# Thirty-two more tokens fetched instead of computed densely, in a decoder step with product-key experts

## The chip, the cores and the metric

The kernel is one program on one NeuronCore of a Trainium2 chip. The number that counts is the device time of one execution in microseconds (us). The engines are PE (TensorE, matrix products), PEld (its weight loads, which run beside the products), DVE (VectorE), ACT (ScalarE), POOL (GpSimd, here nothing but an issuer of indirect DMAs) and SP (SyncE, the issuer of plain DMAs).

## The reference

One decoder layer for 560 token rows: 32 "sample" rows (8 running sequences of 4 tokens, each with 16 cache pages of 128 past tokens) and 528 prompt rows (16 of them meta tokens). What matters here, in outline:

```python
z   = h @ w_in                                # projections
mix = [MLA attention (8 heads), mLSTM (4 heads, 128 x 128 state)] @ w_out
h   = layer_norm(alpha * h + mix)
q   = h @ w_query                             # 8 heads x 2 halves x 128
s1, s2 = q1 @ keys1.T, q2 @ keys2.T           # 128 keys each
top 16 of s1 and s2, top 16 of their 256 sums -> 16 experts of 16384 per head, gates by softmax
y   = sum over the 128 chosen experts e of gate_e * gelu(h . u_e) * v_e
out = layer_norm(alpha * h + y)
```

The experts' tables u and v are 16384 x 1024 in fp32. All outputs (tokens, caches, mLSTM states) are fp32.

## The kernel before

**Two ways to the experts.** The 560 rows stand in five tiles of R = (80, 128, 96, 128, 128) rows; tile 2 (ST) begins with the 32 sample rows. Tiles 0 and 1 are group 0, tiles 2 to 4 group 1. 192 tokens of group 0 (64 of tile 0 and the 128 of tile 1) *fetch* their experts' rows: POOL issues an indirect DMA for one slot of all partitions (`fetch`, L1478: 128 rows of 4 KB, 512 KB), DVE multiplies and sums it with the token (`dot`, L1650 early and L2064 late) and later, for the v rows, scales and adds it (`early_add` L2079, `add_rows` L2071). The 64 tokens stand in the partitions twice, so that they take 64 slots of two experts; tile 1 takes 128 slots. That makes 192 fetches of u rows and 192 of v rows, through a ring of RING = 6 buffers. The 16 meta rows of tile 0 need no output.

The 352 rows of group 1 are computed *densely* against all 16384 experts, in 128 blocks of 128 experts. For each block PE makes the up product (L1024: 8 pieces of the depth x 3 products of rounded and remainder parts, each 352 columns wide), ACT the gelu, DVE `gated` (L2053, times the gates of the block), ACT the rounded part hh, DVE the remainder hl (`low_hidden`, L2057), and PE the down product (L1034: for each of three tiles, three products hh x vh, hh x vl, hl x vh, each in two halves of 512 columns, 18 matmuls in all). ACT rounds u and v (L1129), DVE makes their remainders (`low_u` L2043, `low_v` L2047). The first HS = 24 up products are done early in fp32 (L986), between the gate products.

**The order of the program.** Each engine has its own list, held together by semaphores.

1. Projections (L634), keys and choices of group 0 (`best_keys`, `choose`).
2. Attention of group 1's first tile beside the attention of the samples: `attention(ST, TI - 1, samples=True, each=U_SAMPLE)`. Before it stand `rotate_queries(1)`, `forget_gates(1)` (waits for ACT L1200, L1201) and `sample_queries` (L1618 to L1627, signals qs_ready). For each sample PE computes the scores (L778, L782, L785, L786; the signal is sm_s, for which DVE L1871 waits) and the values (L803 to L809; signal sm_o). After sm_o of sample b the pages of sample b + 2 are loaded: SP loads SP_PAGES = 12 of 16 (L481), POOL gathers the other 4 and 4 pieces of the rotary keys (L1483, L1486), and U_SAMPLE = 5 u rows beside (L1478).
3. `old_states` (mLSTM of the samples) with U_OLD = 11 dots, further tiles, output products with U_OUT = 15, expert queries and keys (L970) with U_KEYS = 24 dots in sets of `best_keys` and 6 dots.
4. Gate stage: for each four tokens DVE makes one-hots (L2036, L2038), PE multiplies them to a matrix of gates (L1011), ACT copies it to a stage buffer (L1129), and SP stores 32 tokens at a time (a chunk, NCH = 11 of them) to a DRAM table `gates`. SP reads it back in quads of four blocks (L521).
5. Down stage and loop: first the 24 early blocks (down products alone, `early_gated` L2085), then 13 turns of 8 blocks (`eight`). Five of the turns have LATE = 18 late dots and 6 adds (24 fetches), eight have 18 adds (18 fetches).
6. Layer norms (LN, L1548 to L1555) of the five tiles on DVE one after the other, each after its residual add (L2232, L2236), and the stores.

Of the kernel before, what the change touches and what calls it, by code (L numbers as in the profile page):

```python
# [6 lines left out]
ALU = mybir.AluOpType  # L7
# [4 lines left out]
U32 = mybir.dt.uint32  # L12
# [9 lines left out]
R = (80, 128, 96, 128, 128)  # L22
T = (0, 80, 208, 304, 432)
# [4 lines left out]
G0 = (0, 208)  # L28
GW = (208, 352)
LAST = (63, 127, 95, 127, 127)  # L30
NF = 64
NH, NOPE, ROPE, VD = 8, 64, 32, 64
# [13 lines left out]
FSETS = (NF, SLOTS)  # L46
RING = 6
CHUNKS = 11
LATE = 18
SP_PAGES = 12  # L50
ITER = LATE * 4 // 3
U_SAMPLE = 5
U_OLD = 11
U_TILE = 4
U_OUT = 15
U_KEYS = 24
U_PRE = SB * U_SAMPLE + U_OLD + 3 * U_TILE + U_OUT + U_KEYS
U_LOOP = 5
HS = 24
HS_GAP = 9  # L60
HS_TURN = 2
V_EARLY = 6 * HS // 8
# [18 lines left out]
HID = 5864  # L81
# [18 lines left out]
assert TS0 + 3592 <= SK0  # L100


def build(nc, x, consts, vecs, lnin, ln1, ln2, wts, w_qb, w_uk, w_uv, sub_keys,
          eu, ev, ur, vr, cache, kpet, pages, ct0, nt0,
          o_y, o_ckv, o_kpe, o_c, o_n, o_m, o_cs, o_ns):
    with ExitStack() as ctx:
# [53 lines left out]
        rstd, rs1, rs4 = small(TI), small(1), small(MH)  # L160
# [22 lines left out]

        hid = view(HID, TI, D)
        lnv = view(LNV, 2, D)
# [16 lines left out]
        class Attention:  # L202

            def __init__(self, at, g):
# [17 lines left out]
                at = max(at, XB + 2 * KD * 512 + 464) if g else at  # L222
# [13 lines left out]
        assert att[0].end <= HTA and att[1].end <= SK0  # L236
# [7 lines left out]
        assert XA + CA <= SK0 and EB + CA + 2 * 544 <= LNV + 2 * D + 64  # L244
# [8 lines left out]
        sc = [view(WQB, 8, NK), view(ZONE, 16, NK)] + [view(ZONE + n * 16 * NK, 16, NK) for n in range(3)]  # L253
        scB = view(ZONE, 3, 16, NK)
        sv = [view(LNV + n * 512, 16, TOPK) for n in (0, 1, 0, 1, 2)]
        siu = [view(LNV + n * 512 + 256, 16, TOPK).bitcast(U32) for n in (0, 1, 0, 1, 2)]
# [8 lines left out]
        cf = view(TS0 + 2944, SLOTS)  # L265
        cb = view(TS0 + 3072, SLOTS)
        ca = view(TS0 + 3200, 2, SLOTS)
        cau = view(TS0 + 3456, SLOTS).bitcast(U32)
# [6 lines left out]
        ZT = XB - 960  # L275
# [15 lines left out]
        assert SCE + D <= ZT  # L291
# [25 lines left out]
        hh = [rounded(f"hh{p}", TS0 + 2 * D + p * GW[1], GW[1])[:, :] for p in range(2)]  # L317
        hl = [rounded(f"hl{p}", TS0 + 2 * D + (2 + p) * GW[1], GW[1])[:, :] for p in range(2)]

        def as32(ap):  # L320
# [15 lines left out]
            "y_ps acc_in out_tok out_state out_y").split()}  # L336
# [26 lines left out]
        def z_bank(at):  # L363
            return 4 + (at - ZB[1]) % 3 if ZB[1] <= at < z_end(1, 4) else at % 4

# [50 lines left out]
        def _(sp):  # L416
# [47 lines left out]
            for n in range(7, 13):  # L464
                chunk(n)
                if n == 9:
                    sp.wait_ge(s["ht_ps"], TI + 1)
                    sp.dma_start(hid[NF:128, 0, :], hid[0:NF, 0, :]).then_inc(s["dup_in"], 16)
# [54 lines left out]

            def load_early_u(pair):
                sp.dma_start(ue[pair % 2].rearrange("p a d -> p (a d)"), eu[pair]).then_inc(early_in[pair % 2], 16)
# [16 lines left out]
            for c in range(NCH):  # L542
# [3 lines left out]
                if c == (T[TI - 1] - S0) // CH + 1:  # L546
# [7 lines left out]
                    load_early_a(1)  # L554
                sp.wait_ge(s["ev_done"], CH // 4 * (c + 1))
                sp.dma_start(gates[c * NK:(c + 1) * NK, :], stage[c % 2].rearrange("p e t -> p (e t)")).then_inc(gs_in[c % 2], 16)
            load_v(1, 1)
            sp.wait_ge(gs_in[0], 16 * ((NCH + 1) // 2))
            sp.wait_ge(gs_in[1], 16 * (NCH // 2))
            for q in range(2):  # L560
                load_gates(q, q)
# [32 lines left out]

            sp.wait_ge(s["f_done"], 2 * sum(FSETS))
            sp.wait_ge(s["y_ps"], NK)
            sp.dma_start(ring[0][0:NF, :], hid[NF:128, 0, :]).then_inc(s["acc_in"], 16)
            for n, i in enumerate((1, 2, 3, 4)):
                sp.wait_ge(s["ln_done"], 2 * TI + n + 1)
                sp.dma_start(o_y[tile(i), :], hid[0:R[i], i, :]).then_inc(s["out_y"], 16)  # L600
            sp.wait_ge(s["ln_done"], 3 * TI)
# [1760 lines left out]
```

## Time and profile before

| what | value |
|---|---|
| median of 3 runs | 2148.72 us (2138.95 to 2148.87) |
| profiled execution | 2147.01 us |
| its span (first to last instruction) | 2145.1 us |
| granted TensorE clock, mean | 0.904 |
| busy: PE, DVE, ACT, POOL | 89%, 67%, 28%, 27% |
| DMA traffic | 479.29 MB, mean 223 GB/s |

The profiled execution is one run with the profiler's records; 1.9 us of its time lie outside the span. Clock 1.00 is 2.4 GHz, 0.5 is 1.2 GHz. A row of the timeline gives start, duration, engine, line, operation, output tile and input tiles, and in brackets the idle time before it and who ended it. "remote" and "another core or an unknown queue" stand where the profile finds no releaser; here there is one core only.

### The profile page before, as it was taken

To read this page: it belongs to the slowest core of one execution; us is meant where nothing else is said; L and a number is where in the kernel's file an instruction comes from. 1 tells how busy PE (TensorE), PEld (TensorE's weight loads), DVE (VectorE), ACT (ScalarE), POOL (GpSimd) and SP (SyncE) were. 2 spreads that over 40 slices of the span, in tenths; PEclk is the share of its full clock that TensorE was granted. 3 is DMA by queue.
4 is the path that set the end of the run, shared out by engine and by line. 5 is a ranking of instruction groups with operands and counts; after the bars stand their busy time and mean duration, and the time that the engine had idled before them with its cause. 6 is when DMAs were issued, how large, how long until landed. Compare 5 with 4: busy or idle time off the path is not lost.

```text
span 2145.1 us, 26500 instructions
## 1 busy us (share of the span) xinstructions
PE 1915.8 (89%) x9117; PEld 1500.0 (70%) x9117; DVE 1436.1 (67%) x3189; ACT 609.1 (28%) x1020; POOL 586.6 (27%) x454
## 2 busy tenths in 40 slices
PE   6988899666688988999886999999999999999994
PEld 3556674554467745667675788888888888888883
DVE  4025366243346755999986778888888777777777
ACT  1132122210011111114455333333333333333331
POOL 0000002344423123310000114454454444444440
PEclk9989999666675679999998999999999999999997
DMA  6611334354534456554438878999998888888872
GB/s 250 228 40 40 123 118 162 108 164 146 186 137 147 148 171 229 202 178 149 164 141 302 295 278 321 356 349 340 364 340 301 317 289 291 320 287 292 318 255 92
DMA packets 152645, 479.29 MB, mean 223 GB/s; under 512 B 14624, under 2 KB 75856, under 8 KB 130928
## 3 DMA queue, kind: packets, MB, share of 16 engines
q1 hardware_dynamic: 94704, 270.60, 34.8%
q0 software_dynamic: 57856, 207.65, 27.2%
q8 instruction: 43, 0.70, 0.1%
q14 instruction: 42, 0.34, 0.0%
HBM read 443.73 MB, written 33.94 MB: 223 GB/s over the span
## 4 chain that ended last, share of the span: by engine, by line
PE 73%; DVE 16%; another core or an unknown queue 4%; DMA 3%; issue 2%; ACT 2%; POOL 0%; SPq 0%; DVEq 0%; ACTq 0%
PE ps L1034 24%; PE ps L1024 19%; PE ps L634 6%; PE ps L970 3%; PE ps L935 3%; PE ps L986 3%; DVE lo L1650 2%; PE ps L1011 2%; PE ps L721 2%; PE ps L720 2%; PE ps L803 2%; PE ps L743 1%; PE ps L638 1%; DMA lo<-x 1%
## 5 line engine op out<-in xcount | busy, mean ns | idle before, releaser
L1478 POOL DMA_INDIRECT lo<-ur,lo x192 | 244.3, 1272 | 797.8 <-DVE lo L2011 323.5
L1478 POOL DMA_INDIRECT lo<-vr,lo x192 | 278.1, 1448 | 650.1 <-DVE lo L2079 306.7
L1024 PE MATMUL ps<-xh,uh 128*128 128x352 f32 x832 | 270.6, 325 | 0.0
L1024 PE MATMUL ps<-xh,ul 128*128 128x352 f32 x832 | 270.5, 325 | 0.0
L1024 PE MATMUL ps<-xl,uh 128*128 128x352 f32 x832 | 268.8, 323 | 0.0
L1129 ACT ACTIVATE hi<-ps 128x512 f32<-128x512 f32 (+10 forms) x259 | 154.3, 645 | 373.7 <-PE ps L970 111.9
L1034 PE MATMUL ps<-vh,hh 128*128 128x512 f32 (+1 forms) x768 | 240.9, 395 | 19.9 <-DVE vl L2047 19.9
L1034 PE MATMUL ps<-vl,hh 128*128 128x512 f32 (+1 forms) x768 | 241.1, 395 | 0.0
L1034 PE MATMUL ps<-vh,hl 128*128 128x512 f32 (+1 forms) x768 | 240.0, 394 | 0.0
L2071 DVE SCALAR_TENSOR_TENSOR lo<-lo 128x1024 f32<-128x1024 f32 x174 | 221.8, 1282 | 18.5 <-DMA lo<-vr,lo 9.7
L2047 DVE TENSOR_TENSOR vl<-hi,vh 128x1024 fp32r<-128x1024 f32 x128 | 156.9, 1226 | 48.8 <-ACT vh L1129 48.3
L1034 PEld LDWEIGHTS ps<-vh,hh 128*128 128x128 f32 (+1 forms) x768 | 138.1, 180 | 48.3 <-issue 20.5
L1129 ACT ACTIVATE hh<-hi 128x352 fp32r<-128x352 f32 x128 | 63.7, 498 | 364.1 <-PE ps L1034 275.1
L1034 PEld LDWEIGHTS ps<-vl,hh 128*128 128x128 f32 (+1 forms) x768 | 138.4, 180 | 39.8 <-issue 0.2
L1034 PEld LDWEIGHTS ps<-vh,hl 128*128 128x128 f32 (+1 forms) x768 | 138.2, 180 | 39.9 <-issue 0.2
L1024 PEld LDWEIGHTS ps<-xl,uh 128*128 128x128 f32 x832 | 156.3, 188 | 4.5
L1024 PEld LDWEIGHTS ps<-xh,uh 128*128 128x128 f32 x832 | 156.3, 188 | 4.3
L2057 DVE TENSOR_TENSOR hl<-hi,hh 128x352 fp32r<-128x352 f32 x128 | 67.3, 526 | 135.2 <-ACT hh L1129 135.2
L1024 PEld LDWEIGHTS ps<-xh,ul 128*128 128x128 f32 x832 | 155.9, 187 | 0.0
L634 PE MATMUL ps<-hi,lo 128*128 128x512 f32 (+5 forms) x320 | 139.0, 594 | 1.1 <-ACT hi L1129 0.7
L1129 ACT ACTIVATE vh<-hi 128x1024 fp32r<-128x1024 f32 x128 | 133.7, 1045 | 7.3 <-DMA gates<-hi 7.3
L970 PE MATMUL ps<-lo,hi 128*128 128x208 f32 (+1 forms) x512 | 130.8, 411 | 2.4 <-ACT lo L1129 2.4
(385 smaller groups left out, 2928.5 us busy)
## 6 DMA issues: line engine op xcount, KB each, us to landing
hi<-ev SPq DMA_DIRECT2D x64, 1024.0 KB
hi<-wts SPq DMA_DIRECT2D x22, 2048.0 KB, 7.8
hi<-eu SPq DMA_DIRECT2D x38, 1024.0 KB, 10.0
lo<-eu SPq DMA_DIRECT2D x26, 1024.0 KB
gates<-hi SPq DMA_DIRECT2D x11, 2048.0 KB, 7.2
hi<-gates SPq DMA_DIRECT2D x32, 704.0 KB, 8.5
lo<-cache SPq DMA_DIRECT2D x48, 128.0 KB
hi<-cache SPq DMA_DIRECT2D x48, 128.0 KB
```

The costliest lines, as they stand in the source:

```text
L634: last = nc.tensor.matmul(ps[0:R[i], bank, 0:w], hT[g][:, k, local(i)], wring[:, n % 2, k, 0:w], start=(k == 0), stop=(k == KD - 1))
L720: nc.tensor.matmul(out, att[g].ql[:, h, local(i)], tt[:, 0, lo:hi], start=True, stop=False)
L935: last = nc.tensor.matmul(ps[0:R[i], m % 4, :], xm[g][:, k, local(i)], wring[:, n % 2, k, :], start=(k == 0), stop=(k == KD - 1))
L970: last = nc.tensor.matmul(ps[:, b % 4, 0:GW[g]], wring[:, n % 2, k, (hp % 4) * 128:(hp % 4 + 1) * 128], hT[g][:, k, :], start=(k == 0), st ...
L986: last = nc.tensor.matmul(ps[:, 5 + 2 * (b % 2), 0:GW[1]], ue[b // 2 % 2][:, b % 2, k * 128:(k + 1) * 128], hT[1][:, k, :], start=(k == 0) ...
L1024: last = nc.tensor.matmul(ps[:, 6 + p, 0:GW[1]], a[p][:, k * 128:(k + 1) * 128], b[:, k, :], start=(k == 0 and b is xh and a is uh), stop= ...
L1034: last = nc.tensor.matmul(ps[0:R[i], 2 * slot(i) + half, :], a[p][:, local(i)], b[p][:, half * 512:(half + 1) * 512], start=(first and a i ...
L1129: return nc.scalar.activation(out, in_, ACT.Copy)
L1478: nc.gpsimd.indirect_dma_start(ring[n % RING], None, table, bass.IndirectOffsetOnAxis(idxs[:, i, k:k + 1], 0)).then_inc(r_in[n % RING], 16)
L2047: v.tensor_tensor(vl[p[1]], vraw[p[0]][:, p[1], :], as32(vh[p[1]]), ALU.subtract).then_inc(s["vl_done"], 1)
L2057: v.tensor_tensor(hl[p], ab[:, p, :], as32(hh[p]), ALU.subtract).then_inc(s["hl_done"], 1)
L2071: v.scalar_tensor_tensor(hid[:, i, :], ring[k % RING], hk[:, i, bass.ds(col, 1)], hid[:, i, :], ALU.mult, ALU.add)\
```

## The change

- **Tokens.** R becomes (112, 128, 64, 128, 128): 32 more prompt tokens move from tile 2 to tile 0 and are fetched. They stand in a tensor of their own, `xq`, in four copies of 32 partitions, which gives them 32 slots of four experts. Fetches of u and v go from 192 to 224 each; the dense width from 352 to 320, the chunks from 11 to 10. A further choice (`QUARTERS`) is made between those of tiles 0 and 1, and for it 16 more key products of 32 rows.
- **Tile 2's down product.** Rounded and remainder part of tile 2's 64 rows stand side by side in `hx`, and are multiplied with vh in one product of 128 columns; 16 matmuls instead of 18. Its two row halves are added up at the end by ACT (yhigh) and two more matmuls. `low_hidden` becomes two DVE instructions.
- **Pages.** SP_PAGES goes from 12 to 9, so POOL gathers 7 pages instead of 4.
- **Dots and adds.** 12 dots (and 12 fetches) between `forget_gates(1)` and `sample_queries`; 6 instead of 5 per sample; 16 instead of 11 in `old_states`; 20 instead of 15 in the output; 36 instead of 24 in the key sets (9 instead of 6 per set); 24 instead of 18 v rows in the early blocks. In the loop five turns have 16 dots and 8 adds, three 24 adds, four 18, the last 16.
- **Direct gates.** The first two quads are read back (chunks 0 to 8) before the last chunk is stored; the last chunk of these two is copied by DVE from the stage buffer.
- **End.** LN of tile 0 and of `xq` stand in the last turn (after block steps 3 and 6), their partial sums are fetched by four DMAs before. The order of the tiles at the end is 0, xq, 1, 3, 4, 2.

```diff
-R = (80, 128, 96, 128, 128)
+R = (112, 128, 64, 128, 128)
-LATE = 18
-SP_PAGES = 12
-ITER = LATE * 4 // 3
-U_SAMPLE = 5
-U_OLD = 11
+LATE = 16
+SP_PAGES = 9
+ITER = LATE * 3 // 2
+U_QUERY = 12
+U_SAMPLE = 6
+U_OLD = 16
...
+                if c == NCH - 1:
+                    for n in range(2):
+                        sp.wait_ge(gs_in[n], stored(n, NCH - 1))
+                    for quad in range(2):
+                        load_first_gates(quad)
...
                 for i in GROUPS[1]:
-                    for a, b in ((hh, vh), (hh, vl), (hl, vh)):
+                    r, c = R[i], local(i)
+                    if i == ST:
+                        products = ((slice(0, 2 * r), hx[p][:, 0:2 * r], vh), (slice(0, r), hh[p][:, c], vl))
+                    else:
+                        low = hl[p][:, c.start - LOW:c.stop - LOW]
+                        products = ((slice(0, r), hh[p][:, c], vh), (slice(0, r), hh[p][:, c], vl), (slice(0, r), low, vh))
+                    for n, (m, a, b) in enumerate(products):
                         for half in range(2):
...
             load_pages(0)
+            u_fetches(RING, RING + U_QUERY)
             pool.wait_ge(s["qs_ready"], 1)
             load_pages(1)
...
+            best_keys(QUARTERS, 0)
             choose(0)
+            choose(QUARTERS)
             choose(1)
 
-            dve.wait_ge(s["dup_in"], 16)
+            dve.wait_ge(s["dup_in"], 80)
             rotate_queries(1)
             forget_gates(1)
+            dots(0, U_QUERY)
             sample_queries()
-            attention(ST, TI - 1, samples=True, each=U_SAMPLE)
-            at = SB * U_SAMPLE
+            attention(ST, TI - 1, samples=True, at=U_QUERY, each=U_SAMPLE)
+            at = U_QUERY + SB * U_SAMPLE
...
             dve.wait_ge(s["gm_ps"], GW[1] // 4)
+            low_v((0, 0), 1)
+            fetched_gates(0)
+            dve.wait_ge(gs_in[1], stored(1, NCH))
+            dve.wait_ge(s["ev_done"], GW[1] // 4)
+            for quad in range(2):
+                ins = v.tensor_copy(gt[quad][:, NCH - 1], stage[staged(NCH - 1)][:, quad * 4:quad * 4 + 4, :])
+            step(ins)
             early_gated(0)
             low_hidden(0, 1)
-            low_v((0, 0), 1)
-            fetched_gates(0)
...
             def low_hidden(p, n):
                 dve.wait_ge(s["hh_done"], n)
-                v.tensor_tensor(hl[p], ab[:, p, :], as32(hh[p]), ALU.subtract).then_inc(s["hl_done"], 1)
+                v.tensor_tensor(hx[p][:, 0:LOW], ab[:, p, 0:LOW], as32(hh[p][:, 0:LOW]), ALU.subtract)
+                v.tensor_tensor(hl[p], ab[:, p, LOW:GW[1]], as32(hh[p][:, LOW:GW[1]]), ALU.subtract).then_inc(s["hl_done"], 1)
...
+                    if final and q == LN_AT[0]:
+                        dve.wait_ge(s["ln2_in"], 16)
+                        dve.wait_ge(s["acc_in"], 64)
+                        step(v.tensor_tensor(hid[0:NF, 0, :], hid[0:NF, 0, :], halves[0:NF, :], ALU.add))
+                        layer_norm(hid[:, 0, :], 0, 2 * TI)
+                    if final and q == LN_AT[1]:
+                        for part in quarters:
+                            step(v.tensor_tensor(xq[0:NV, :], xq[0:NV, :], part[0:NV, :], ALU.add))
+                        layer_norm(xq, TI, 2 * TI + 1)
```

What stands in the engines' lists at three places:

PE, one block's down product at the end of the program before (vh, vl: rounded v rows and their remainder; ps: the sums of the three tiles).

```order
L1034 MATMUL ps<-vh,hh 96x512 x2
L1034 MATMUL ps<-vl,hh 96x512 x2
L1034 MATMUL ps<-vh,hl 96x512 x2
L1034 MATMUL ps<-vh,hh 128x512 x2
L1034 MATMUL ps<-vl,hh 128x512 x2
L1034 MATMUL ps<-vh,hl 128x512 x2
```

PE, the same block in the changed kernel, of which the last three rows stand twice as they did before.

```order
L1084 MATMUL ps<-vh,hx 128x512 x2
L1084 MATMUL ps<-vl,hx 64x512 x2
L1084 MATMUL ps<-vh,hx 128x512 x2
L1084 MATMUL ps<-vl,hx 128x512 x2
L1084 MATMUL ps<-vh,hl 128x512 x2
```

Tile 2's three pairs have become two, and the first of them reads the remainder that DVE writes into hx.

POOL, two samples' bursts before: cache pages, rotary keys, u rows.

```order
L1483 DMA lo<-cache,lo 128x256 x4
L1486 DMA lo<-kpet,lo 128x128 x4
L1478 DMA lo<-ur,lo 128x1024 x5
L1483 DMA hi<-cache,lo 128x256 x4
L1486 DMA lo<-kpet,lo 128x128 x4
```

POOL, the same place in the changed kernel.

```order
L1551 DMA lo<-cache,lo 128x256 x7
L1554 DMA lo<-kpet,lo 128x128 x4
L1546 DMA lo<-ur,lo 128x1024 x6
L1551 DMA hi<-cache,lo 128x256 x7
L1554 DMA lo<-kpet,lo 128x128 x4
```

A burst has 17 gathers where it had 13.

DVE, from the end of `forget_gates(1)` into `sample_queries` before.

```order
L1641 COPY lo<-ps 128x4 x2
L1643 TENSOR_TENSOR lo<-lo 128x12
L1618 COPY hi<-hi 32x8x32 x4
L1621 TENSOR_SCALAR hi<-hi 128x256
L1624 MEMSET hi 128x1024
L1627 TENSOR_SCALAR hi<-ps 32x8x32 x4
```

DVE, the same place in the changed kernel (a dot is two rows of L1722; eleven more like it are left out).

```order
L1712 COPY lo<-ps 128x4 x2
L1714 TENSOR_TENSOR lo<-lo 128x12
L1722 ISA lo<-lo 128x1024
L1722 ISA lo 128x1
...
L1689 COPY hi<-hi 32x8x32 x4
L1692 TENSOR_SCALAR hi<-hi 128x256
L1695 MEMSET hi 128x1024
L1698 TENSOR_SCALAR hi<-ps 32x8x32 x4
```

Twelve dots stand ahead of the four instructions for which the samples' scores wait.

## Rows read from the trace of the kernel before

**Rows 1.** The page: busy time, share of the span and instructions of the engines.

```profile
PE 1915.8 (89%) x9117; PEld 1500.0 (70%) x9117; DVE 1436.1 (67%) x3189; ACT 609.1 (28%) x1020; POOL 586.6 (27%) x454
```

**Rows 2.** The page: the chain that ended last, shares of the span.

```profile
PE 73%; DVE 16%; another core or an unknown queue 4%; DMA 3%; issue 2%; ACT 2%; POOL 0%; SPq 0%; DVEq 0%; ACTq 0%
```

**Rows 3.** Windows: PE, PEld, DVE, ACT, POOL busy (count), clock, DMA share, GB/s.

```profile
1332.50:1397.00 64.50, 64.50 (x338) 57.30 (x337) 54.48 (x76) 22.91 (x32) 32.17 (x24) 1.00 0.96 348
1719.00:1783.60 64.60, 64.60 (x338) 57.37 (x338) 48.91 (x50) 22.90 (x32) 27.94 (x19) 1.00 0.83 299
1376.00:1380.00 4.00, 4.00 (x21) 3.32 (x20) 3.41 (x6) 1.41 (x2) 2.31 (x2) 1.00 1.01 416
```

**Rows 4.** The chain in the loop and at its end: start, us, what.

```profile
1272.35 4.18 PE ps L1034 x18
1276.53 3.92 PE ps L1024 x24
...
2114.09 1.29 DVE lo L2071
2115.41 1.30 DVE lo L1548 x2
```

**Rows 5.** Waits in 1268:1590: total, times, longest.

```profile
DVE hl L2057 <- ACT hh L1129: 31.0, 30, 2.1
...
DVE lo L2071 <- DMA lo<-vr,lo: 8.4, 7, 1.8
```

**Rows 6.** Groups by shape, the whole run: busy us, mean ns, idle before.

```profile
L970 PE MATMUL ps<-lo,hi 128*128 128x352 f32 x256 | 80.8, 471 | 1.2 <-ACT lo L1129 1.2
L1011 PE MATMUL ps<-hi 128*128 128x128 f32 x704 | 93.0, 289 | 19.8 <-DVE hi L2038 17.3 <-ACT hi L1129 1.4
```

**Rows 7.** The chain in 960:1172: shares by line, and its end.

```profile
by line: PE ps L986 25.9%; PE ps L1011 20.3%; DVE hi L2036 9.5%; DVE hi L2038 9.1%; issue 8.1%; DMA gates<-hi 6.4%; DVE lo L1985 4.1%; DVE hi L1984 3.4%; DVE hi L2026 2.2%; DVE hi L1936 1.5%; ACT hi L1129 1.2%; DVE hi L2023 1.2%; DVE hi L20
1135.42 13.48 DMA gates<-hi
```

**Rows 8.** Timeline of the same end, and the first down product.

```profile
1163.50 1.17 SPq L521 DMA_DIRECT2D hi<-gates  x2
...
1171.63 1.14 PE L1034 MATMUL ps<-vh,hh 128*96 128x512 f32 x2 [17.60 <-DVE vl L2047]
```

**Rows 9.** Timeline of DVE before the samples' attention.

```profile
307.64 0.87 DVE L1921 MAX8 lo<-hi 128x8 f32<-128x128 f32 x4
...
354.88 0.20 DVE L1991 RECIPROCAL lo<-lo 128x8 f32<-128x8 f32 x1
...
382.38 0.17 DVE L1638 TENSOR_TENSOR lo<-lo 128x12 f32<-128x12 f32 x1 [21.14 <-ACT lo L1201]
```

**Rows 10.** Timeline of one sample: SP, POOL, and DVE's next score.

```profile
446.41 8.90 SPq L481 DMA_DIRECT2D hi<-cache  x12
446.50 0.94 POOL L1483 DMA_INDIRECT hi<-cache,lo  x1 [1.57 <-PE ps L809]
...
452.10 0.25 PE L785 MATMUL ps<-hi 128*32 128x32 f32 x2
...
459.01 0.93 POOL L1478 DMA_INDIRECT lo<-ur,lo  x1 [0.30 <-issue]
462.26 0.69 DVE L1871 TENSOR_REDUCE lo<-ps 128x32 f32<-128x512 f32 x1 [13.71 <-remote]
```

**Rows 11.** Waits of DVE in 393:606.

```profile
DVE lo L1871 <- remote: 81.3, 6, 14.3
```

**Rows 12.** The chain in 640:935: dots (two rows each in the count).

```profile
643.32 1.15 DVE lo L1650 x2
...
658.50 1.23 DVE lo L1650 x2
...
877.15 6.96 DVE lo L1650 x12
...
899.66 6.96 DVE lo L1650 x12
```

More of the change, by code:

```diff
@@ L364, in z_bank, with turn, staged, stored @@
             return 4 + (at - ZB[1]) % 3 if ZB[1] <= at < z_end(1, 4) else at % 4
+        QUARTERS = TI
+        CHOICES = (0, QUARTERS, 1, 2, 3, 4)
+        FINAL = (0, QUARTERS, 1, 3, 4, 2)
+        LN_AT = (3, 6)
+        def turn(i):
+            return CHOICES.index(i)
+        def staged(c):
+            return (c + NCH + 1) % 2
+        def stored(n, c1):
+            return 16 * sum(staged(c) == n for c in range(c1))
         def tile(i):
@@ L467, in _ @@
                     sp.wait_ge(s["ht_ps"], TI + 1)
+                    for c in range(4):
+                        sp.dma_start(xq[c * NV:(c + 1) * NV, :], hid[NF:NF + NV, 0, :]).then_inc(s["dup_in"], 16)
+                    sp.wait_ge(s["dup_in"], 64)
                     sp.dma_start(hid[NF:128, 0, :], hid[0:NF, 0, :]).then_inc(s["dup_in"], 16)
@@ L554, in _ @@
                     load_early_a(1)
+                if c == NCH - 1:
[3 more added lines that the diff above has]
+                        load_first_gates(quad)
                 sp.wait_ge(s["ev_done"], CH // 4 * (c + 1))
-                sp.dma_start(gates[c * NK:(c + 1) * NK, :], stage[c % 2].rearrange("p e t -> p (e t)")).then_inc(gs_in[c % 2], 16)
+                sp.dma_start(gates[c * NK:(c + 1) * NK, :], stage[staged(c)].rearrange("p e t -> p (e t)")).then_inc(gs_in[staged(c)], 16)
             load_v(1, 1)
[L558 to L561, printed above, removed]
+            for n in range(2):
+                sp.wait_ge(gs_in[n], stored(n, NCH))
             for b in range(HS):
@@ L995, in gate_products @@
                     r = R[i]
-                    pe.wait_ge(s["tk_pick"], i + 1)
+                    pe.wait_ge(s["tk_pick"], turn(i) + 1)
                     if i > ST:
@@ L1115, in _ @@
             eight((NK - HS) // 8 - 1, final=True)
+            pe.wait_ge(s["yh_done"], 1)
+            r = R[ST]
+            for half in range(2):
+                last = nc.tensor.matmul(ps[0:r, half, :], ident[r:2 * r, r:2 * r], yhigh[r:2 * r, half, :], start=False, stop=True,
+                                        skip_group_check=True)
+            last.then_inc(s["y_ps"], 1)
         @block.scalar
@@ L1463, in _ @@
             eight((NK - HS) // 8 - 1, final=True)
-            for n, i in enumerate((1, 2, 3, 4, 0)):
-                root(i, 2 * TI + n)
+            for n, i in enumerate(FINAL):
+                if n >= 2:
+                    root(i, 2 * TI + n)
+                if i == 1:
+                    act.wait_ge(s["y_ps"], NK)
+                    r = R[ST]
+                    copy(yhigh[r:2 * r], ps[r:2 * r, 0:2, :]).then_inc(s["yh_done"], 1)
         @block.gpsimd
@@ L2210, in _ @@
                     v.tensor_tensor(xl, hT[1], as32(xh), ALU.subtract).then_inc(s["xl_done"], 1)
-                for k in range(6 * (b % 8) // 8 + 6 * (b // 8), 6 * (b % 8 + 1) // 8 + 6 * (b // 8)):
-                    early_add(k)
-            eight_dots(0, first=True)
-            with dve.Fori(1, U_LOOP) as j:
+                early_add(b)
+            with dve.Fori(0, U_LOOP) as j:
                 eight_dots(j)
```

260 lines of the change are left out of this document (150 added, 110 removed).

## The prediction

> **What bounds the kernel now.** I read the page first. PE is busy for 89% of the span [rows 1], and the chain that ended last runs through PE for 73% and through DVE for 16% [rows 2]. So a change counts where PE sets the pace, and elsewhere where DVE or an unknown releaser stands in the chain. I then read the windows of two loop turns: PE is busy for all of both, 64.5 us, at clock 1.00, while DVE works 54.5 us in a turn with 24 fetches and 48.9 in one with 18; the DMA engines move 348 and 299 GB/s, at shares of 0.96 and 0.83 [rows 3]. The loop is PE's, with DMA and DVE close behind in the first kind. From the loop's chain I took the price of a block [rows 4], from its waits the slack of DVE [rows 5], from the groups by shape the products of other widths [rows 6]. Then I followed the chain through the stages that the change touches: gates [rows 7, 8], start of the samples' attention [rows 9], one sample [rows 10, 11], dots on the chain [rows 12].
>
> **The dense work.** A block before is 3.92 us of up (24 matmuls, 163 ns each, 352 columns) and 4.15 of down (the mean of 4.18 and 4.12; 18 matmuls, 231 ns, 512 columns) [rows 4]. The two durations give a slope of 0.42 ns per column, so 320 columns take 149 ns and the up product 3.58 us; 16 down matmuls take 3.69. With 128 down and 104 up products in the stage: 128 x 0.46 + 104 x 0.33 = 93 us less. Does the weight load, which stays 128 columns wide, hold it up? L1011 has 704 matmuls with weights as wide in 93.0 us, 132 ns each [rows 6], below 149. **Term -93.**
>
> **What stands against it in the loop.** A turn becomes 58.2 us (8 x 7.27). A turn with 24 fetches moves 348 x 64.5 = 22.4 MB [rows 3]; in 58.2 us that is 385 GB/s, and there are eight such turns now instead of five. DVE's adds are the second claim: a turn with 18 adds costs DVE 48.9 us; adds are 1.33 apart (five in 6.7 us, from 2108.73 on), so 24 cost 57 of the 58.2. DVE also waits 31.0 us for ACT's hh in 40 blocks [rows 5], time that it could use only in part. The lower bound is nothing: one window of 4 us shows 416 GB/s [rows 3]. The upper bound is that the turns stay as long as they are, 8 x 6.3 = 50. The 8.4 us of DMA waits in five turns [rows 5] show that the present rate already lets a transfer be late, and all of it was hidden; I take 2 us per turn. **Term +15** (0 to 50).
>
> By the Trainium skill (DMA: Bandwidth & Descriptors, Where 436 GB/s comes from) transfers from HBM are bound at about 358 GB/s per core. By it, the eight turns would need 62.6 us, +35 instead of +15. The window of 416 GB/s speaks against it as a hard bound over 4 us [rows 3]; no row here shows such a rate over 60.
>
> **Gate stage.** 80 groups of four tokens instead of 88. L2036, L2038 and L1011 hold 38.9% of a chain of 212 us [rows 7]; an eleventh is 7.5. L986 holds 25.9%, 55 us, and gets 9% fewer columns: 5. **Term -12** (-16 to -7).
>
> **Start of the down stage.** After the last gate product SP stores the last chunk, reads two quads back at 1163.50, and PE begins at 1171.63, having stood 17.6 us [rows 8]. With the direct gates the read-back lies ahead of the last store, and what is left on the path is ACT's last copy, DVE's copies of the chunk, gated, hh, hl: some 7 us by the pieces from 1168.73 on plus the copies. But the read-back must wait for the store before, whose like held the chain for 13.48 us [rows 7]. **Term -10** (-13 to -3).
>
> **End.** From the last down product DVE does five LN and their adds before [rows 4], and five after; the adds of the quarters are three instead of one. LN of tile 0 is new in the last turn, where DVE has 0.4 us per block to spare: 5.4 us (1.2 + 4.2), of which PE loses 4. The tail itself: 33.8 against 32.9 by the same durations. **Term +5** (0 to +9).
>
> **Widths in between.** L970 for group 0 grows by 32 columns: 32/352 x 80.8 = 7 [rows 6], for group 1 it shrinks by as much, of which the first key set's part is hidden; the key copies add 2, the other products about nothing. **Term +5** (0 to +9).
>
> **Start of the samples' attention.** DVE's keys and choices run from 307.64 to 355.4 before: a set of best_keys and 12 heads [rows 9]. A set takes 5.2 (between two sets of dots 22.5 - 7.0 = 15.5 for three [rows 12]), so a head takes 3.5, and the new choice 5.2 + 7.1 = 12.3, up to 15.7 with its fixed part. It is hidden: DVE then waits 21.14 us for ACT's L1201 [rows 9]; but ACT in turn waits for PE, which needs the turned queries, and there I count 12 us of slack; so +5. The 12 dots are not hidden at all: behind them stand the queries of the samples, their scores, POOL's load_pages(1) (it waits for qs_ready) and the whole attention. Six rows are there at 1.16 each (6.96 for six [rows 12]), the other six come at the pace of fetches after the dots, as in old_states (11 dots in 16.4 us [rows 12]): 18, less 4.4 that DVE waits there anyway. **Term +19** (+8 to +24).
>
> **One sample.** PE's scores are recorded until 452.35, yet DVE's L1871 resumes at 462.26 without a releaser that the profile knows [rows 10]. This happens in six of eight samples, 81.3 us in all [rows 11]. The resumption comes 2.3 us behind POOL's last gather of the burst (459.01 + 0.93) [rows 10], the same offset within 0.2 in all six. If POOL's burst is what delays it, three more pages and one more u row at 1.25 us each (12.5 us for 10 gathers [rows 10]) cost 5.0 per sample. If it is SP's 12 loads of 8.9 us, nine loads are shorter and it gains 2 per sample. I take the first, since its offset is the steadier. **Term +30** (-12 to +36).
>
> **Dots on the chain.** old_states: five more dots by the same pace, 16.4 / 11 x 5 = 7.5, and the output steps' 2.3 to 4; together **+12**. The key sets: three more dots, 3.5 us, three to four times, all on the chain [rows 12]: **+13**.
>
> **Sum.** -93 + 15 - 12 - 10 + 5 + 5 + 19 + 30 + 12 + 13 = -16, from the profiled 2147.0: **2131 us**. That execution is 1.7 below the median of 2148.7, so the sum against the median would be 2133; I keep 2131, which lies 0.8% below it. What a measurement of this kernel can tell from no change is about 0.5%, 10.7 us.
>
> **Rivals.**
> - *The samples pay nothing* (chance 0.2). PE's signal comes late through something that the page gathers don't lengthen. For it: no semaphore in the program ties L1871 to POOL's burst. Against: the steady offset. Then 2131 - 30 = 2101, or 2090 if SP's loads set it.
> - *The loop keeps its pace* (0.2), the case on the other side. The place is the eight turns with 24 fetches: if fetched rows arrive at no more than 348 GB/s, each lasts 64.4 instead of 58.2. Price 50 instead of 15: 2166, slower. It decides from about 350 GB/s down; at 358, by the Trainium skill's rule (same page and section), it is 2151, no change. For it: the share of 0.96. Against: windows of 416.
> - *The hidden sides are not hidden* (0.1). The first up or down product of a block waits for DVE, because tile 2's first product now reads DVE's remainder in hx, not only ACT's hh; DVE is at 57 of 58.2 in the turns of 24 adds. One us per block in three turns: +24, 2155, no change to slower.
> - *My forecast* (0.5): 2131, own range 2115 to 2146.
>
> **How the numbers follow.** Faster by over 0.5% means below 2138. The forecast's range lies there for 0.34 of its 0.5, the first rival wholly, 0.2, the others with 0.02: 0.56. Same: 0.15 of the forecast, 0.06 of the loop's case, 0.05 of hidden sides: 0.26. Slower: 0.18. The range of 8 in 10 reaches into the first rival and into the loop's: 2092 to 2162.
>
> **What the changed profile would show.** Loop blocks of 7.27 us on the chain and turns of 58.2 us, with DMA at 385 GB/s; if the turns with 24 fetches last over 61, the loop's rival holds, and the waits name DMA or DVE. L1871 resuming 2.3 us behind POOL's last gather, some 5 us later after sm_o than before: my term; unchanged or earlier: the first rival. 18 us of dots ahead of sample_queries with PE idle. The first down product within 8 us of the last gate product. Wrong would make me above all a loop limited by transfers, or a sample stage that does not follow POOL.

## The result, and the profile after

The changed kernel takes **2167.97 us** (median of 4 runs, 2164.5 to 2171.7) against 2143.88 us of the kernel before, measured beside it (4 runs, 2138.95 to 2148.87). The ratio is 1.0113, 95% interval 1.0076 to 1.015: slower by 1.1%. The forecast was 2131, range 2092 to 2162. The profiled execution took 2167.24 us, its span is 2165.4. The ratios of the experiments leave out three slow executions, 8429.87 us of a_18, 2726.3 of a_keys and 2092.74 of best1_b.

The page after, parts 1 and 4:

```profile
PE 1846.5 (85%) x8833; PEld 1421.8 (66%) x8833; DVE 1523.7 (70%) x3494; ACT 603.6 (28%) x1033; POOL 693.8 (32%) x542
PE 61%; DVE 18%; DMA 6%; issue 5%; another core or an unknown queue 5%; ACT 3%; POOL 2%; SPq 0%; DVEq 0%; ACTq 0%
```

PE works 69 us less than in [rows 1], yet the span is 20.3 us longer. On the chain [rows 2] PE has lost 12 points of its share; most of them went to DMA, issue, DVE and POOL. So the work saved was real and something else grew.

The table has the length of each stage, from the start or end of an instruction that stands in both kernels (the same program line). `waits for ACT` ends with the DVE instruction behind the 21 us wait in [rows 9]; `queries` with the last of sample_queries; `samples` is from the first to the last score (L1871 before); `tiles` ends with the last product of the values of attention (L743 before), `output` with L935, `expert queries` with L970, `keys` with the first L1011, `gates` with the last L1011, `start` with the first down product, `early blocks` with the first up product of the loop, `loop` with the last down product. "c1" and "c2" are two levels of absolute time at which groups of runs came out (see the experiments); c1 has the profiles before and after, c2 before_b and after_b.

```
stage            before  after  diff |  before  after  diff
                     c1     c1       |      c2     c2
waits for ACT     382.4  414.2 +31.8 |   383.8  415.8 +32.0
queries            10.0   24.3 +14.3 |    10.0   24.6 +14.6
first score        12.3   16.6  +4.3 |    12.3   12.2  -0.1
samples           201.9  215.5 +13.6 |   142.8  155.1 +12.3
tiles             157.4  175.7 +18.3 |   143.4  175.4 +32.0
output             56.6   59.0  +2.4 |    58.8   58.8   0.0
expert queries     99.1  105.6  +6.5 |    98.7  106.5  +7.8
keys               61.2   83.8 +22.6 |    61.2   83.0 +21.8
gates             173.1  171.5  -1.6 |   174.9  171.4  -3.5
start              17.6    4.0 -13.6 |    16.4    4.1 -12.3
early blocks       96.7  100.5  +3.8 |    98.0  100.6  +2.6
loop              846.0  761.5 -84.5 |   846.0  760.5 -85.5
end                30.8   33.3  +2.5 |    30.8   33.4  +2.6
```

The loop gives what was asked of it. Its chain after (start, us, what), and three of its stretches (columns as in [rows 3]):

```profile
1370.77 3.53 PE ps L1068 x24
1374.30 3.66 PE ps L1084 x16
1377.96 3.53 PE ps L1068 x24
```

```profile
1536.00:1594.00 58.00, 58.00 (x326) 51.89 (x325) 54.94 (x82) 22.83 (x33) 31.04 (x25) 1.00 1.02 396
1710.00:1768.00 58.00, 58.00 (x326) 51.89 (x325) 56.23 (x68) 23.41 (x33) 34.93 (x25) 1.00 1.02 396
2000.00:2058.00 58.00, 58.00 (x324) 51.76 (x322) 49.13 (x59) 23.00 (x34) 27.77 (x19) 1.00 0.93 332
```

A block is 7.19 us (7.27 were forecast), PE is busy for all of each stretch, and DMA carries 396 GB/s over 58 us in the first two. The bound of about 358 GB/s for transfers from HBM that the Trainium skill gives (DMA: Bandwidth & Descriptors, Where 436 GB/s comes from) does not show here, where one core is at work: these two rows are 11% above it for a whole turn each.

The loss stands ahead of the loop: the first down product begins at 1270.1 instead of 1171.6 [rows 8], 98.5 us later, where the forecast's terms make 57. Three places show in the trace. ACT and PE at the second group's projections:

```profile
353.69 0.23 ACT L1368 ACTIVATE hi<-hi 128x32 f32<-128x32 f32 x1 [12.42 <-DVE hi L2038]
353.83 1.74 ACT L1184 ACTIVATE hi<-ps 128x128 f32<-128x128 f32 x6
354.58 0.48 PE L694 MATMUL ps<-lo,hi 128*128 128x128 f32 x1 [11.45 <-issue]
```

L1368 is the line of the choices' exponentials, here that of the new choice. It stands in ACT's list ahead of the copies of PE's transposes (L1184), waits 12.4 us for DVE, and PE stands 11.45 us for the copies. The chain in the key sets (L1722 is the dot):

```profile
1007.68 5.25 DMA lo<-ur,lo
1012.95 1.23 DVE lo L1722 x2
...
1029.73 1.24 DVE lo L1722 x2
1031.23 7.86 DMA lo<-ur,lo
1039.11 1.23 DVE lo L1722 x2
```

The ring has six rows. Of nine dots in a set the seventh can be fetched only once the first is done; the sets shown stop for a transfer. Waits of DVE from the end of the tiles to the first gate product (846:1095):

```profile
DVE lo L1990 <- PE ps L976: 23.1, 2, 21.4
DVE lo L1998 <- ACT hi L1184: 20.1, 1, 20.1
DVE lo L1722 <- DMA lo<-ur,lo: 18.0, 10, 5.1
```

And one early block (timeline):

```profile
1289.03 1.28 DVE L2163 SCALAR_TENSOR_TENSOR lo<-lo 128x1024 f32<-128x1024 f32 x1
...
1290.23 0.49 DVE L2169 TENSOR_TENSOR hi<-lo,hi 128x320 f32<-128x320 f32 x1
...
1290.75 0.47 ACT L1184 ACTIVATE hx<-hi 128x320 fp32r<-128x320 f32 x1 [5.62 <-DVE hi L2169]
...
1292.20 1.23 DVE L2130 TENSOR_TENSOR vl<-hi,vh 128x1024 fp32r<-128x1024 f32 x1 [0.39 <-ACT vh L1184]
...
1293.57 0.71 PE L1084 MATMUL ps<-vh,hx 128*128 128x512 f32 x2 [3.14 <-DVE vl L2130]
```

Add, gates, ACT, remainder and vl follow one another: 4.31 us a block by the distance of the adds on the chain, where PE needs 3.66.

### The profile page after: what moved, and what is told of

Same layout as the page of the kernel before. It is cut to its first block, busy times and chain, and to the rows that moved or that the text cites. A ratio compares the mean times of both kernels' runs of the same rounds, so it can differ in the third digit from the quotient of the medians.

```text
span 2165.4 us, 26334 instructions
## 1 busy us (share of the span) xinstructions
PE 1846.5 (85%) x8833; PEld 1421.8 (66%) x8833; DVE 1523.7 (70%) x3494; ACT 603.6 (28%) x1033; POOL 693.8 (32%) x542
## 4 chain that ended last, share of the span: by engine, by line
PE 61%; DVE 18%; DMA 6%; issue 5%; another core or an unknown queue 5%; ACT 3%; POOL 2%; SPq 0%; DVEq 0%; ACTq 0%
PE ps L1084 17%; PE ps L1068 16%; PE ps L675 5%; PE ps L1014 4%; DMA lo<-ur,lo 3%; PE ps L1030 2%; PE ps L1055 2%; DVE lo L1722 2%; POOL lo L1546 2%; PE ps L976 2%; PE ps L784 2%; PE ps L762 2%; PE ps L761 1%; PE ps L679 1%
## 5 line engine op out<-in xcount | busy, mean ns | idle before, releaser
L1068 PE MATMUL ps<-xh,uh 128*128 128x320 f32 x832 | 258.6, 311 | 4.1 <-DVE ul L2126 4.1
L1184 ACT ACTIVATE hi<-ps 128x512 f32<-128x512 f32 (+11 forms) x251 | 146.6, 626 | 404.1 <-PE ps L1014 108.7
L1068 PE MATMUL ps<-xl,uh 128*128 128x320 f32 x832 | 257.7, 310 | 0.0
L1068 PE MATMUL ps<-xh,ul 128*128 128x320 f32 x832 | 257.3, 309 | 0.0
L1084 PE MATMUL ps<-vh,hx 128*128 128x512 f32 x768 | 241.4, 395 | 17.1 <-DVE vl L2130 13.1
L1084 PE MATMUL ps<-vl,hx 128*128 128x512 f32 (+1 forms) x768 | 238.9, 392 | 0.0
L1084 PEld LDWEIGHTS ps<-vh,hx 128*128 128x128 f32 x768 | 138.9, 189 | 53.7 <-issue 26.1
L1084 PE MATMUL ps<-vh,hl 128*128 128x512 f32 x512 | 158.1, 390 | 0.0
L1722 DVE CUSTOM_DVE_ANT_0 lo<-lo 128x1024 f32<-128x1024 f32 x112 | 131.0, 1222 | 21.9 <-DMA lo<-ur,lo 20.7
L1184 ACT ACTIVATE hx<-hi 128x320 fp32r<-128x320 f32 x128 | 60.5, 473 | 299.2 <-PE ps L1084 173.6
L1184 ACT ACTIVATE vh<-hi 128x1024 fp32r<-128x1024 f32 x128 | 133.8, 1046 | 0.0
L1014 PE MATMUL ps<-lo,hi 128*128 128x240 f32 (+1 forms) x512 | 131.1, 411 | 2.3 <-ACT lo L1184 2.3
```

The costliest lines, as they stand in the source:

```text
L1014: last = nc.tensor.matmul(ps[:, b % 4, 0:GW[g]], wring[:, n % 2, k, (hp % 4) * 128:(hp % 4 + 1) * 128], hT[g][:, k, :], start=(k == 0), st ...
L1068: last = nc.tensor.matmul(ps[:, 6 + p, 0:GW[1]], a[p][:, k * 128:(k + 1) * 128], b[:, k, :], start=(k == 0 and b is xh and a is uh), stop= ...
L1084: last = nc.tensor.matmul(ps[m, 2 * slot(i) + half, :], a, b[p][:, half * 512:(half + 1) * 512], start=(first and n == 0), stop=(final and ...
L1184: return nc.scalar.activation(out, in_, ACT.Copy)
L1722: v.tensor_tensor_reduce(ring[n % RING], ring[n % RING], rows, 1.0, 0.0, ALU.mult, ALU.add, adot[:, i, k:k + 1])\
```

## The experiments

Every ratio is to the kernel before, timed in the same group of runs on the same chip. Absolute times differ between the groups. The record numbers the chips:

| group | chip | median of before | level |
|---|---|---|---|
| first comparison (before, after) | not recorded | 2143.9 | c1 |
| a_exp, a_early, a_pages12, b_pages9 | 9 | 2077.0 | c2 |
| before_b, after_b, a_18, best1 | 5 | 2079.9 | c2 |
| a_keys, a_old, a_nogates, a_noln | 9 | 2135.6 | c1 |
| a_old0, best1_b, best2 | 14 | 2145.7 | c1 |

Number 9 stands beside both levels, so the level does not go with the chip's number; what sets it is open. Stages are compared within a level.

**1. before_b and after_b: both kernels again.** No edit.

> The kernel before, unchanged, for a second profile on the chip of this group, since absolute times differ from chip to chip. Theory 1 (the unexplained waits of the samples are a property of the run, not of the program): from the first to the last score about 150 us, where the first profile has 201.9; all other stages as in the first profile within 2 us. Rival (they are the program's): 202 us again.

> The changed kernel, unchanged, for a profile beside that of the kernel before on the same chip. It stays slower than before by 1.0 to 1.5%. The samples' scores span 155 us (215.5 in the first profile) if the waits belong to the chip.

Measured: before 2078.9, after 2102.2, ratio 1.0100 (1.0070 to 1.0129). The samples span 142.8 and 155.1 us instead of 201.9 and 215.5, and the waits of DVE in them (393:552) read:

```profile
DVE lo L1871 <- PE ps L786: 36.7, 8, 8.7
DVE hi L1673 <- PE ps L721: 24.5, 13, 3.0
```

The 81.3 us of waits without a releaser [rows 11] are gone, with the same program and the same bursts of POOL. So a burst alone does not make them; how they arise stays open, but they go with the level. In the samples the change costs 12 to 14 us at both.

Does the answer follow POOL's last gather where the waits exist, as the prediction took it? The changed kernel's profile at c1 has two of its samples like this (timeline; DVE's score among POOL's gathers of pages, and behind its last gather, of a u row):

```profile
538.68 0.95 POOL L1551 DMA_INDIRECT lo<-cache,lo  x1 [0.31 <-issue]
539.39 0.69 DVE L1948 TENSOR_REDUCE lo<-ps 128x32 f32<-128x512 f32 x1 [5.93 <-remote]
539.93 0.95 POOL L1551 DMA_INDIRECT lo<-cache,lo  x1 [0.30 <-issue]
...
612.27 0.94 POOL L1546 DMA_INDIRECT lo<-ur,lo  x1 [0.30 <-issue]
615.90 0.69 DVE L1948 TENSOR_REDUCE lo<-ps 128x32 f32<-128x512 f32 x1 [19.06 <-remote]
```

Once DVE resumes in the middle of the page gathers, once 2.7 us behind the end of the last gather. The steady 2.3 us of the first profile is not there, and the first of these two answers did not wait for the burst to end.

**2. Pages.** a_pages12: `SP_PAGES = 12` in the changed kernel. b_pages9: `SP_PAGES = 9` in the kernel before.

> The changed kernel with 12 pages by SP and 4 by POOL, as before. Theory 1 (POOL's burst sets when the next sample's score is answered): each of six samples is 3 x 1.25 us shorter, 22 us in all. Rival A (the whole traffic of pages and fetched rows sets it, whoever issues it): no difference over 3 us. Rival B (SP's queue sets it): 5 to 15 us longer, which is what the change would have gained by nine pages.

> The kernel before with 9 pages by SP and 7 by POOL, nothing else changed. Theory 1 (POOL's burst): from the first to the last score of the samples 201.9 us becomes 224, the execution 22 us longer, 2166. Rival A (traffic): no difference. Rival B (SP's queue): 5 to 15 us shorter.

Measured on c2: a_pages12 1.0092 (1.0075 to 1.0109), samples 150.8 instead of 155.1; b_pages9 1.0084 (1.0051 to 1.0116), samples 149.5 instead of 142.8. So three pages more on POOL cost 4.3 to 6.7 us of the samples, a third to a fifth of what their issue time would make: at c2 theory 1 falls, and so do both rivals in b_pages9 (no difference; shorter). The timed runs don't tell a_pages12 from the changed kernel (1.0100); b_pages9 is 17 us longer than before, more than its samples. Another 9.4 us of its profile lie in the tiles, a stage whose program the edit doesn't touch (see 6). At c1, where the waits exist, no run varies the pages alone.

**3. a_exp.**

```diff
+            token_copies(1)
             softmax_exp(QUARTERS, 2)
-            token_copies(1)
```

> The changed kernel with one line moved: the exponential of the new choice stands behind the copies of the second group's transposes in ACT's list, not ahead of them. Theory 1 (ACT waits 12.4 us in front of that exponential, and PE stands 11.5 us for the copies behind it, all on the path): the last L675 product ends 11 to 13 us earlier, the execution is 11 us shorter than the changed kernel, about 2157. Rival (the projections there have slack, or DVE's choice becomes the last arrival instead): under 3 us. Kept from the change: everything else.

Measured: 1.0084 (1.0067 to 1.0101), the first stage 408.5 instead of 415.8. PE's stop of 11.45 us is gone, but a new one stands a little later (timelines: the transposes' products that had stopped, then PE and ACT in 366:384):

```profile
344.57 0.60 PE L696 MATMUL ps<-lo,hi 128*128 128x128 f32 x4
345.01 0.28 PE L694 MATMUL ps<-lo,hi 128*128 128x128 f32 x1
...
372.96 6.02 PE L711 MATMUL ps<-hi 128*128 128x320 f32 x16 [5.97 <-issue]
...
372.07 0.31 ACT L1368 ACTIVATE hi<-hi 128x128 f32<-128x128 f32 x1 [11.31 <-DVE hi L2038]
372.29 0.58 ACT L1184 ACTIVATE hi<-ps 128x512 f32<-128x512 f32 x1
```

The next exponential on ACT's list, that of tile 1, now waits 11.31 us for DVE, and PE stands 5.97 us, where it stood 0.73 in the changed kernel, until the copy behind it is done. So the mechanism holds, and it moved on by one choice, which is in part the rival: DVE's choices became the last arrival. So 7.3 us and not 11 came back in the profile; best1 has the same stop of 5.94 us. The same stage differed by 4.5 us between after_b and a_18, which share its program, and the timed runs (1.0084 against 1.0100 of after_b) don't tell a_exp from the changed kernel. The rest of this stage's +32 stands mostly ahead of it: in the changed kernel the second group's projections begin at 319.39, in the kernel before at 302.38, 17 us.

**4. a_keys.** With `KEY_DOTS = (18, 6, 6, 6)`:

```diff
-                dots(at, at + U_KEYS // 4)
-                at += U_KEYS // 4
+                dots(at, at + KEY_DOTS[q0 // 4])
+                at += KEY_DOTS[q0 // 4]
```

> The changed kernel with its 36 dots of the key sets dealt as 18, 6, 6 and 6 instead of four times 9. Theory 1 (the ring has six rows, so that the seventh to ninth dot of a set wait for a fetch that could start only after the first dot; the first set has a wait of 20 us behind it that covers more dots): from the end of the output products to the first gate product 15 to 22 us shorter. Rival (the dots cost what they cost, 1.16 us each, wherever they stand on DVE's list): 3 x 3 x 1.16 = 10 us shorter.

Measured: 1.0023 (1.0001 to 1.0045); keys 62.3 instead of 83.8, expert queries 105.9 instead of 105.6. Nine dots moved, 21.5 us gained in the stage: 2.4 us a dot, not 1.16. The timed runs agree, 0.9% or 19 us from 1.0113 (the profile's span is 26.8 shorter, against a profile of another group). Theory 1 holds. In front of the first set, DVE's wait for ACT is now

```profile
DVE lo L1999 <- ACT hi L1185: 3.6, 1, 3.6
```

instead of 20.1, so the nine stand where DVE had waited.

**5. a_early.**

```diff
                 else:
                     gated(0, 2 * HS + 16, 1)
+                early_add(b)
...
-                early_add(b)
```

> The changed kernel with the early blocks' add standing between the gates' product and the remainder of the hidden (so that ACT's rounding runs beside the add), not at the end of the block. Theory 1 (the 24 early blocks last 4.31 us each because DVE's add, gates, ACT's hx, remainder and vl follow one another): they fall to PE's 3.67 us, 24 x 0.64 = 15 us less, about 2153. Rival (fetched rows arrive too late for a block of 3.67 us, the ring being the limit): no change, DVE waits for DMA instead.

Measured: 1.0093 (1.0059 to 1.0128); early blocks 94.1 instead of 100.6. Late in the stage the chain has no DVE any more, and PE runs in one piece (the window of this view, 1240:1290, ends inside it):

```profile
1243.40 13.48 DMA hi<-ev
...
1259.37 30.75 PE ps L1084 x127
```

Order was the cause, but 6.5 us came back and not 15: PE still waits three times for vl, 8.2 us in all, once behind a load of v. The timed runs (1.0093 against 1.0100) don't tell 6.5 us from nothing.

**6. a_old and a_old0.** `U_OLD = 11` and `U_OLD = 0`, the dots in front of the first key set.

> The changed kernel with 11 dots in old_states as before, and the other five in front of the first key set, where DVE waits 20 us. Theory 1 (the five dots wait for fetches that follow one another at 1.5 to 2 us, and PE stands for them): from the last sample's score to the end of the last tile's values, 175 us, becomes 165. Theory 2 (this stage has grown by 32 us because PE ran it at a granted clock of 0.5, where before it had 0.5 to 1.0): little of it, under 5 us, unless the clock changes with it.

> The changed kernel with no dot in old_states; its 16 stand in front of the first key set, where only about 11 of them are covered. Theory 1 (dots between the last sample's score and the last tile's values are on the path): that stage, 173 to 176 us in three profiles of this program part, falls by 16 us or more, and the key stage grows by 5 to 10. Theory 2 (PE at half its clock is the stage's pace, and gaps filled with dots don't matter): under 6 us, and the length follows the granted clock: 0.52 went with 184 us, 0.59 with 175, 0.69 with 143.

Measured: a_old 1.0103 (1.0068 to 1.0138), a_old0 1.0022 (1.0011 to 1.0033). By the timed runs sixteen dots are worth 0.9% and five next to nothing. In the profiles the tiles take 184.2 us with 11 dots and 171.3 with none, 175.7 with 16; for a_old0 the keys grow by 7.2. Both profiles are of the slowest execution of their kernel (2179.43 us where the other four of a_old took 2158 to 2162; 2162.44 where the median of a_old0 is 2150.6), so the single profile of a_old is no typical one. The windows of exactly this stage (columns as in [rows 3]; before, before_b, after, a_old, a_old0):

```profile
606.60:764.00 157.40, 138.76 (x607) 110.66 (x607) 104.96 (x347) 29.72 (x76) 32.92 (x28) 0.62 0.41 141
```

```profile
548.90:692.30 143.40, 127.90 (x607) 101.93 (x607) 101.28 (x335) 29.73 (x76) 31.50 (x28) 0.69 0.45 152
```

```profile
670.50:846.20 175.70, 149.68 (x607) 111.39 (x604) 110.80 (x355) 29.50 (x76) 41.14 (x34) 0.59 0.41 144
```

```profile
677.40:861.60 184.20, 168.86 (x605) 123.33 (x603) 107.42 (x351) 29.50 (x76) 33.55 (x29) 0.52 0.38 127
```

```profile
669.70:841.00 171.30, 158.08 (x607) 117.95 (x607) 94.70 (x329) 29.50 (x76) 18.96 (x18) 0.56 0.30 101
```

The same 607 matmuls cost PE 128 us at a mean granted clock of 0.69 (a mixture of stretches at 1.2 and at 2.4 GHz) and 169 at 0.52 (nearly all of the stage at 1.2 GHz). A least-squares line through the 15 profiles of both groups gives 1.8 us for each hundredth of clock, 0.8 us for each dot in old_states and 10 us for being a version of the changed kernel, with nothing over 5 us left over. By this line the stage's growth at c1, 18.3 us, is 5 of clock (0.62 to 0.59), 4 of dots and 10 that no run here took apart; at c2, 32 us, it is 18 of clock (0.69 to 0.59), 4 and 10. The line describes the profiles; it does not show whether the lower clock lengthens the stage or the longer stops lower the clock. So neither theory is shown alone.

**7. a_18.** Tile 2's down product as three products again, and without the adding of its halves at the end (not in this excerpt).

```diff
-                        products = ((slice(0, 2 * r), hx[p][:, 0:2 * r], vh), (slice(0, r), hh[p][:, c], vl))
+                        products = ((slice(0, r), hh[p][:, c], vh), (slice(0, r), hh[p][:, c], vl), (slice(0, r), hx[p][:, 0:r], vh))
```

> The changed kernel with tile 2's down product made as three products of 64 rows again (18 matmuls a block instead of 16), and without the two matmuls that add its halves at the end. Theory 1 (a block costs PE what its matmuls cost, 231 ns each): 104 blocks x 0.46 = 48 us longer in the loop and little in the early blocks, which DVE bounds. Rival (DVE or the transfers bound the loop at 7.2 us a block): under 15 us longer.

Measured: 1.0324 (1.0255 to 1.0393); the loop 805.8 instead of 760.5, the early blocks unchanged. Two matmuls less a block are worth 45.3 us in the loop (48 by PE's price), and all of it is PE's:

```profile
1402.14 3.53 PE ps L1068 x24
1405.67 4.12 PE ps L1084 x18
```

**8. a_nogates.** Without `load_first_gates` and DVE's copies; `load_gates(q, q)` for both after the last store.

> The changed kernel without the direct gates: both first quads are read back whole after the last chunk's store, as before. Theory 1: from the last gate product to the first down product 4.1 us becomes 14 to 17, the execution 11 us longer. Rival (other work ahead of the down stage, the rounding of v and the adds' gates, was the last arrival): under 3 us.

Measured: 1.0184 (1.0140 to 1.0228); start 15.2 instead of 4.0, early blocks 96.9 instead of 100.5, loop 756.9 instead of 761.5, all of it in the last turn. The direct gates give 11.2 us at the start; the early blocks take 3.6 back, and what the last turn differs by was not looked into. The ratio is 0.7% above 1.0113, 15 us. The samples of this profile are 13 us longer, and they stand ahead of the edit, so the ratio may overstate it.

**9. a_noln.** The two layer norms after the loop, with ACT's part of them.

```diff
-                    if final and q == LN_AT[0]:
...
             dve.wait_ge(s["f_done"], 2 * NU)
+            dve.wait_ge(s["ln2_in"], 16)
+            dve.wait_ge(s["acc_in"], 64)
...
             layer_norm(hid[:, 1, :], 1, 2 * TI + 2)
```

> The changed kernel with the layer norms of tile 0 and of xq after the loop instead of in its last turn. Theory 1 (in the last turn DVE is near PE's pace, so that their 5.4 and 7.9 us were only partly free): the tail from the last down product is 9 us longer and the last turn 4 us shorter, 5 us in all. Rival (the last turn hid them whole): 9 to 13 us longer. Rival (PE lost all of it): no change.

Measured: 1.0125 (1.0078 to 1.0173); loop 754.9 instead of 761.5, end 38.5 instead of 33.3. Moved into the last turn the two norms save 5.2 us of tail and cost up to 6.6 of loop (other profiles with the norms in the last turn have loops of 756.9 to 762): nothing gained that can be measured.

**10. best1 and best2: the dots where DVE waits.** The early down blocks now carry 24 dots (not adds), all turns but the last 24 fetches:

```diff
-V_EARLY = HS
+U_EARLY = HS
...
+                dot(U_PRE + b)
...
-                early_add(b)
...
+            U_AT = U_PRE + U_EARLY
...
-            u_fetches(at, U_PRE)
-            n = U_PRE
-            for b in range(V_EARLY):
-                fetch(n, vr, 0, b)
-                n += 1
+            u_fetches(at, U_AT)
+            n = U_AT
...
-U_QUERY = 12
-U_OLD = 16
-U_OUT = 20
-U_KEYS = 36
+U_QUERY = 0
+U_OLD = 11
+U_OUT = 15
+U_KEYS = 34
```

The new dot stands between the gates' product and the remainder, the key sets are 16, 6, 6 and 6, with the exponential moved as in a_exp and 12 pages by SP. best2 has 5 dots per sample, 5 in old_states, 12 ahead of `output` and key sets of 18, 6, 6, 6.

> The changed kernel with what the two traces point to: 24 of the u rows fetched and multiplied in the early down blocks (where the adds stood) and all turns but the last with 24 fetches, so that only 120 dots stand ahead of them: none before the samples' queries, 11 in old_states, 15 in the output, key sets of 16, 6, 6 and 6; the early dot between gates' product and remainder; the new choice's exponential behind the copies; 12 pages by SP. Theory 1 (the change loses its gain by work put on the path ahead of the loop): against the changed kernel 11 (exponential) + 14 (queries) + 7 to 10 (old_states) + 3 (output) + 15 to 20 (keys) + 15 (early blocks) + 5 (pages) = 70 to 78 us shorter, 2 to 2.5% faster than before. Rival (the transfers can't carry 24 fetches in seven turns of adds, or the fetches in the early blocks are late): 30 us of it are lost in the loop.

> The best version so far again, beside its successor on the same chip. If its gain doesn't depend on the chip, the ratio to the kernel before is 0.966 to 0.977 as measured first; on a chip where PE answers the samples late it could lose a part: 0.98.

> best1 with 5 dots per sample and 5 in old_states, and the 14 so freed placed where DVE waits anyway: 12 ahead of the first output product (21 us wait for the weights' load and PE there) and 2 more in the first key set. Theory 1 (a dot costs nothing where DVE waits and fetches have time): 4 us less in the samples, 5 to 9 less in old_states, output and keys unchanged: 9 to 13 us shorter than best1. Rival (the fetches' traffic delays the output weights): under 3 us.

Measured: best1 **0.9714** (0.9659 to 0.9769) on c2, 0.9653 (0.9611 to 0.9696) on c1; best2 **0.9657** (0.9634 to 0.9679) on c1. Against after_b the span of best1 is 81 us shorter: first stage 7.7, queries 15.3, samples 8.4, tiles 9.7, expert queries 10.1, keys 20.9, early blocks 8.2, the loop 0.6 longer. The forecast was 70 to 78; its rival, 30 us lost in the loop, did not come. Several edits are in it together, so a stage's gain is not each edit's own. That the loop bears it shows in a turn of adds:

```profile
1780.00:1838.00 58.00, 58.00 (x325) 51.90 (x324) 56.15 (x65) 23.21 (x34) 33.44 (x25) 1.00 1.00 390
```

best2 is no faster than best1: in its profile tiles take 153.7 instead of 168.5, samples 206.2 instead of 198.0 and expert queries 101.5 instead of 95.9. Its freed dots moved work about, and the timed runs don't tell the two apart.

## Why the prediction was wrong

The sign was wrong and the time lay 6 us above the range. In the profiles the span grew by 20 us where the sum had -16. By its steps:

- *The dense work, -93, and +15 against it*: right in sum, in part by luck. Early blocks and loop together went from 942.7 to 862.0, -80.7, where -78 stood. Within it the parts differ: the turns with 24 fetches paid nothing (the term +15 was 0) and a block costs 7.19 and not 7.27, while 12 us were lost in the early blocks (100.5 where 24 x 3.66 is 88; ordering returned 6.5 in a_early) and up to 6.6 us to the norms in the last turn. a_18 confirms the price of a matmul.
- *The rival "the loop keeps its pace"* named 2166, close to what was measured, by a mechanism that is refuted: each of the first twelve turns took PE's 57.5 us.
- *The rival "the hidden sides are not hidden"* put its waits into the loop's turns, where none show; in the early blocks PE does wait for DVE.
- *Start, -10*: -13.6, near its edge of -13. *End, +5*: +2.5 in the tail and up to 6.6 in the loop, so 9 at the range's edge. *The twelve dots, 14 of +19*: 14.3.
- **The step that failed is the sum of the work ahead of the loop**: +57 forecast, +98.5 measured. The terms that were too low:
  - *Start of the samples' attention* without the dots, 5, and *widths*, 5: 31.8. The new choice was costed on DVE's list alone; that its exponential stands on ACT's list in front of PE's copies was not looked for (PE's stop of 11.45 us; 7.3 came back in the profile of a_exp). The second group's projections begin 17.0 us later. Of that 7.0 are the wider queries of group 0 (0.44 in each of 16 key steps), as forecast. The key products of the new choice, which the term put at about nothing, are 0.34 more in each step, 5.4 in all, and 4.4 stand ahead of the steps.
  - *Dots on the chain*: a dot was priced at 1.16 us. In the key sets of nine the last three cost 2.4 each (a_keys), since the ring holds six rows and the rest wait for a transfer. Keys and expert queries: +29.1, where 13 stood. The keys' +22.6 is what a_keys gives back; the 6.5 of the expert queries no run isolates.
  - *old_states, 7.5*: the stage grew by 18 at c1 and 32 at c2. Dots are some 4 of it. The part that goes with the clock and the 10 us that no run explains (see 6) had no term.
  - *Gates, -12*: -1.6. The chain's last store of a chunk is 15.47 us of `gates<-hi` where it was 13.48 [rows 7]. That the stores now set this stage's pace is a reading of the chain, which no run tested; why the rest of the saving is missing stays open.
- *One sample, +30*, was too high: 13.6. Its mechanism, the next score following POOL's last gather, failed too: the offset is not steady in the changed kernel's own profile, and before_b has the same bursts without the wait. The term was twice too large and so, by luck, hid 16 us of the other errors. The rival that the samples pay nothing did not come either.

## What to carry to other kernels

Work moved off the bounding engine must be priced where it lands: count the instructions per stretch against the depth of the ring that feeds them, and look at what stands behind each new wait on *every* in-order list that it touches, not only on the list that does the new work. A stage before the loop where DVE, PE and ACT hand over to one another has little cover, but for the places where DVE waits for something else; best1, which took 24 dots out of there and put them into the early blocks, gained in both. An offset that is steady over six repeats of one profile shows no cause; a second profile of the same kernel had none of the waits.

## What the runs showed of the hardware that was not expected

- The same program took 2077 to 2080 us in two groups of runs and 2136 to 2146 in three, and chip number 9 had both. In the profiles, of the 68 us of span between the two levels 59 lie in one stage (201.9 against 142.8 us). In it DVE's scores resumed 9.2 to 10.3 us behind PE's last recorded matmul of the score, in six waits (81.3 us of idle DVE) while pages and rows were loaded; at the other level they resumed within 0.04 us. Another 14 us lie in the next stage; all others together are 5 us longer at the faster level.
- A stage with PE busy for 83 to 92% of it was granted between 0.52 and 0.69 of the clock, from profile to profile of nearly the same instructions, and took 184 to 143 us.
- DMA carried 373 to 396 GB/s at shares of 0.99 to 1.02 in seven stretches of 58 us in a row (after, 1420 to 1826), without PE losing anything.
